# Four more half-size product groups, and a retention stage of four units per head, in a one-core decoder step

## The chip, the cores and the metric

The kernel runs on one core of a Trainium2 chip. The metric is the device time of one execution in microseconds (us), lower is better. In the names of the profile PE is the matrix engine (TensorE), PEld its weight loads, DVE the vector engine, ACT the scalar engine, POOL GpSimd and SP the engine whose queue issues most DMAs.

## What is computed

The reference is one inference step of a hybrid decoder layer for 1024 prompt tokens and 8 sample tokens (1032 token columns together), D_MODEL 1024. Cut to what matters here:

```python
hn   = rms_norm(x, norm_mix)
proj = hn @ w_in                                  # 7424 columns
rq, rk, rv, rg, aq, ak, av, gr, ga = split(proj)  # 512, 512, 1024, 1024, 3 x 768, 2 x 1024
# retention, 4 heads, keys of 128, values of 256, chunks of 128 tokens
for chunk: scores = (q @ k.T) * decay
           o  = scores @ v + (q @ state) * inner
           state = state * gamma**128 + (k * tail).T @ v
o = group_norm(o) * silu(rg)                      # per head, gates of 256 columns
r_branch = o @ w_ret_branch
# then dilated attention (3 groups), gated merge, output projection, SwiGLU FFN, final norm
```

The 8 samples do one retention step each, from a stored state of 128 x 256 per head, and that state is updated and written out.

## The kernel before

Activations lie transposed, features on the 128 partitions and 1032 tokens along the free axis. A product with a float32 weight is made of three fp32r products (high x high, high x low, low x high): POOL splits each weight into a high and a low part, ACT or DVE the activations.

Work on PE comes in two forms.

A **unit** (`unit`, L996) makes 128 output columns of a projection: 8 contraction steps k, each of 9 matmuls of 344 tokens, 72 matmuls. Two PSUM buffers `unit_ps` alternate, and so do two weight buffers. DVE takes a finished unit out of PSUM in `scaled` (times `rstd`), which frees the buffer (`unit_free`). POOL splits the weights of unit n (`split`, L864 and L867, 128x1024 each) when unit n-2 is done; SP loads them (`load`) when the split of unit n-2 is done.

A **half** (`in_half`, `product`, L1057) makes 256 output columns by seven products of half-size matrices instead of eight (Strassen-Winograd): 7 x 4 x 3 x 2 = 168 matmuls of 258 tokens. ACT snapshots and DVE combines the results into `temp` or `h_out`, DVE scales by `rstd`, SP stores 1032 KB to `att_spill`. IN_TURNS = 3 turns of two halves make the queries, keys and values of attention groups 0 and 1.

After the halves come the four units of U_HEAD0 (head 0: two of values, keys, queries), then four heads. Under head h six units run: values, keys and queries of head h+1 and the two units of head h's gates `rg`. Between their k steps PE does the **28 tasks** of head h's retention, placed by the table RET_AT: `(j, k): x` puts task x ahead of step k of unit j. Tasks by number: VT 0 to 3, VS 4 (values turned to token order), KT_ 5, 6, KS 7 (keys), SC 8, 9 (scores), UP 10 to 13 (state products), OUT_ 14 to 17 (outputs), OUTER 18 to 21 and OS 22 (samples), TURN 23 to 26 and TS 27 (outputs turned back). Tasks alternate between two PSUM banks: a task waits until the one two before it has been emptied (`task_free`), by ACT for VT, VS, KS, OUT_, OS, by DVE for the others. Instructions on an engine are executed in order, so a task that waits holds up the unit behind it.

DVE and ACT walk through `ret_slot(.., j)` for j = 0 to 5, each followed by taking unit j out. Of DVE's slots these matter:

- slot 1: scores, q times inner, then UP; slot 2 begins once `scaled` has taken unit 1, with UP+3 and then the **sample preparation**: casts s_khigh and s_vparts (L2217, L2219), s_klow, s_vparts (L2221, L2222), three s_kparts (L2225) and s_qmask (L2227), which signals `masked_ready`. PE's first OUTER task waits for it.
- slot 3: statistics and normalisation of the outputs (L2245 to L2260), which signals `normed` for TURN.
- slot 4: the turned outputs are copied into `wide`; in `gated` the two gate units are scaled into `stage`, put through Silu by ACT, and multiplied in (L2283).

ACT's slot 2 empties the four OUT_ tasks. The last head's tasks run in the six units of attention group 2 (U_GROUP2); there ACT does `spill(j)` after its slot j: it waits until DVE has taken unit j and issues a DMA.

The lines on which the order rests:

```python
RET_AT.update({(1, 0): 6, (1, 1): 7, (1, 2): 8, (1, 3): 9, (1, 5): 10, (1, 6): 11, (1, 7): 12, (2, 0): 13})
RET_AT.update({(2, 1 + j): 14 + j for j in range(7)})
RET_AT.update({(3, 0): 21, (3, 3): 22, (4, 4): 23, (4, 5): 24, (4, 6): 25, (4, 7): 26, (5, 1): 27})
```

Of the kernel before, what the change touches and what calls it, by code (L numbers as in the profile page):

```python
# [29 lines left out]
ALU = mybir.AluOpType  # L30
# [4 lines left out]
P = 128  # L35
# [30 lines left out]
U_HEADS = U_HEAD0 + 4  # L66
U_GROUP2 = U_HEADS + 6 * (HEADS - 1)
# [20 lines left out]
IN_TURNS = 3  # L88
# [45 lines left out]
RET_AT = {(0, 2 + j): j for j in range(6)}  # L134
RET_AT.update({(1, 0): 6, (1, 1): 7, (1, 2): 8, (1, 3): 9, (1, 5): 10, (1, 6): 11, (1, 7): 12, (2, 0): 13})
RET_AT.update({(2, 1 + j): 14 + j for j in range(7)})
RET_AT.update({(3, 0): 21, (3, 3): 22, (4, 4): 23, (4, 5): 24, (4, 6): 25, (4, 7): 26, (5, 1): 27})

STEPS_HEAD = 29
# [141 lines left out]
def build(nc, a, out):  # L281
    ctx = ExitStack()
    with ctx:
# [136 lines left out]
        att_spill = scratch("att_spill", [18, P, TOKENS])  # L420
# [49 lines left out]
        x_again = sem("x_again")  # L470
        window = sem("window")
# [86 lines left out]
        def in_columns(t, x):  # L558

            g, kind = divmod(2 * t + x, 3)  # L560
            return COL_ATT + KIND * kind + 2 * P * g, 6 * g + 2 * kind
# [28 lines left out]
        def _(sp):  # L590
# [43 lines left out]
            for t in range(IN_TURNS):  # L634
                if t == 1:
                    sp.dma_start(x_late[:], x_spill[0:KH, :, second].rearrange("k p t -> p k t")).then_inc(x_again, 16)
                for x in range(2):
                    half = 2 * t + x
                    sp.wait_ge(part_split, PRODUCTS * (half + 1))
                    if t + 1 < IN_TURNS:  # L640
                        in_load(x, (raw_a, raw_b)[x], t + 1)
                    elif x == 0:
                        for j, c in enumerate((COL_RV, COL_RV + P)):
                            load(Place(U_HEAD0), j, KT, w_in[:, :, c:c + P])
                    if half >= 1:
                        in_store(*IN_HALVES[half - 1])

            in_store(IN_TURNS - 1, 1)
            sp.wait_ge(product_done, LAST_IN + PRODUCTS)
            for j, c in enumerate((COL_RK, COL_RQ)):  # L650
                load(Place(U_HEAD0), 2 + j, KT, w_in[:, :, c:c + P])
# [3 lines left out]
            with sp.Fori(0, HEADS - 1) as h:  # L655
                for j, (c, by) in enumerate(((COL_RV + DV, DV), (COL_RV + DV + P, DV), (COL_RK + DK, DK),
                                             (COL_RQ + DK, DK), (COL_RG, DV), (COL_RG + P, DV))):
                    load(Place(U_HEADS, 6, h), j, KT, w_in[:, :, ds(h * by + c, P)])
            for j in range(6):
                c = COL_ATT + 2 * 256 + KIND * (j // 2) + P * (j % 2)  # L660
                load(Place(U_GROUP2), j, KT, w_in[:, :, c:c + P])
            for j in range(2):
                c = COL_RG + 3 * DV + P * j
                load(Place(U_GATE3), j, KT, w_in[:, :, c:c + P])
# [313 lines left out]
        def _(pe):  # L978
# [129 lines left out]
            for j in range(1, 4):  # L1108
                unit(Place(U_HEAD0), j, KT, a_hi, a_lo)


            def ret_task(pl, up, heads, j):


                ps = begin(pl, j)
                if j == 0:

                    pe.wait_ge(unit_free[0], up.half(0))
                    pe.wait_ge(unit_free[1], up.half(0))
# [44 lines left out]
                elif j == OS:  # L1164

                    taken(pl, OUTER + 3)
# [16 lines left out]
                end(mm, j)  # L1183

            def ret_stage(pl, up, heads):
                for j in range(6):
                    unit(up, j, KT, a_hi, a_lo,
                         between=lambda k: ret_task(pl, up, heads, RET_AT[j, k]) if (j, k) in RET_AT else None)

            with pe.Fori(0, HEADS - 1) as h:  # L1190
                ret_stage(Place(T_RET, RET_TASKS, h), Place(U_HEADS, 6, h), h)
            ret_stage(Place(T_RET + RET_TASKS * (HEADS - 1)), Place(U_GROUP2), HEADS - 1)

# [262 lines left out]
        def _(act):  # L1456
# [165 lines left out]
            def ret_slot(pl, h, j):  # L1622

                for x in {0: range(VT, KT_), 1: (KS,), 2: range(OUT_, OUTER), 3: (OS,)}.get(j, ()):
                    ps = full(pl, x)
# [11 lines left out]
                    empty(ins, x)  # L1637
                if j == 2:

                    act.wait_ge(task_free[1], pl.half(UP + 3) + 1)  # L1640
                    act.dma_start(out["p_ret"][0, 0][ds(h, 1)].rearrange("a d v -> d (a v)"), states[:, CHUNKS - 1, :])\
                       .then_inc(p_stored, 16)
                if j == 3:

                    act.wait_ge(task_free[0], pl.half(OUTER + 2) + 1)
                    act.wait_ge(task_free[1], pl.half(OUTER + 3) + 1)
# [7 lines left out]
            with act.Fori(0, HEADS - 1) as h:  # L1654
                pl = Place(T_RET, RET_TASKS, h)
                up = Place(U_HEADS, 6, h)
                for j in range(6):
                    ret_slot(pl, h, j)
                    if j >= 4:
                        in_place(up, j, ACT.Silu)  # L1660

                act.wait_ge(s_stored, h * 16 + 16)
                load_states(h + 1)
# [6 lines left out]
            for j in range(6):  # L1670
                ret_slot(Place(T_RET + RET_TASKS * (HEADS - 1)), HEADS - 1, j)
# [163 lines left out]
            act.dma_start(s_qkv_t[:], att_spill[:, :, SEQ:TOKENS].rearrange("a p t -> p a t")).then_inc(qkv_loaded, 16)  # L1835
# [198 lines left out]
        def _(dve):  # L2034
# [140 lines left out]
            scaled(Place(U_HEAD0), 0, v_t[:, 0, :])  # L2175
            scaled(Place(U_HEAD0), 1, v_t[:, 1, :])
            scaled(Place(U_HEAD0), 2, k_t[:])
            scaled(Place(U_HEAD0), 3, q_t[:], DK ** -0.5)
            dve.wait_ge(table_loaded, 16 * 2)

            def ret_slot(pl, h, j):

                if j < 2:

                    empty(dve.tensor_scalar(k_tok[:, 4 * j:4 * j + 4, :],
                                            full(pl, KT_ + j)[:].rearrange("p (q d) -> p q d", q=4),
                                            const("tail")[:, ds(h, 1)], None, ALU.mult), KT_ + j)
                if j == 1:
                    for x in range(2):
                        ps = full(pl, SC + x)[:].rearrange("p (q t) -> p q t", q=4)  # L2190
                        empty(dve.tensor_tensor(scores_t[:, 4 * x:4 * x + 4, :], ps,
                                                decay[:, ds(h, 1), :].to_broadcast([P, 4, P]), ALU.mult), SC + x)
# [3 lines left out]
                if j in (1, 2):  # L2196
                    for x in (range(UP, UP + 3) if j == 1 else (UP + 3,)):
                        ps = full(pl, x)
                        for q in range(2):
# [11 lines left out]
                            else:  # L2211
                                empty(ins, x)
                                dve.wait_ge(task_free[x % 2], pl.half(x) + 1)
                if j == 2:
                    dve.wait_ge(task_free[KS % 2], pl.half(KS) + 1)
# [14 lines left out]
                if j in (2, 3):  # L2230
                    for x in (range(OUTER, OUTER + 3) if j == 2 else (OUTER + 3,)):
                        if x == OUTER:
# [3 lines left out]
                        ps = full(pl, x)[:].rearrange("p (q d) -> p q d", q=2)  # L2236
                        empty(dve.scalar_tensor_tensor(out=s, in0=s, scalar=const("gamma")[:, ds(h, 1)], in1=ps,
                                                       op0=ALU.mult, op1=ALU.add), x)
                if j == 3:

                    for x in (OUT_ + 2, OUT_ + 3, OS):
                        dve.wait_ge(task_free[x % 2], pl.half(x) + 1)
# [19 lines left out]
                if j == 4:  # L2262

                    dve.wait_ge(p_stored, h * 16 + 16)

                    for x in range(4):
                        ps = full(pl, TURN + x)[:].rearrange("p (v t) -> p v t", v=2)
                        empty(dve.tensor_copy(wide[:, ds(h * 2, 2), 2 * P * x:2 * P * (x + 1)], ps), TURN + x)
                    ps = full(pl, TS)[:, 0:2 * SAMPLES].rearrange("p (v t) -> p v t", v=2)
                    empty(dve.tensor_copy(wide[:, ds(h * 2, 2), SEQ:TOKENS], ps), TS)  # L2270
# [4 lines left out]
            def gated(pl, j, h, v, done):  # L2275

                scaled(pl, j, stage[:, j % 2, :])
                dve.wait_ge(silu_done, done)

                for b in range(2):  # L2280
                    dve.wait_ge(task_free[b], h * (RET_TASKS // 2) + (T_RET + RET_TASKS) // 2)
                t = flat(wide[:, ds(h * 2 + v, 1), :])
                step(dve.tensor_tensor(t, t, stage[:, j % 2, :], ALU.mult))  # L2283

            with dve.Fori(0, HEADS - 1) as h:
                step.enter(h, STEPS_HEAD)
                up = Place(U_HEADS, 6, h)
                for j in range(6):
                    ret_slot(Place(T_RET, RET_TASKS, h), h, j)
# [4 lines left out]
                    elif j == 3:  # L2294
                        scaled(up, j, q_t[:], DK ** -0.5)
                    else:
                        gated(up, j, h, j - 4, h * 2 + (U_HEAD0 + j - 3))
                step.leave(HEADS - 1)

            for j in range(6):  # L2300
                ret_slot(Place(T_RET + RET_TASKS * (HEADS - 1)), HEADS - 1, j)
# [457 lines left out]
```

## Time and profile before

| what | value |
|---|---|
| time, median of 3 runs | 1776.24 us (1775.83 to 1776.53) |
| profiled execution, its own time | 1775.5 us |
| its span, first to last instruction | 1773.7 us |
| PE busy | 1749.7 us (99%) |
| DVE, ACT, POOL busy | 828.6, 496.8, 920.8 us |
| halves, 73 to 194.4 us | PE busy throughout |
| retention stage, 194.4 to about 600 us | PE busy throughout |

A start in a timeline is the first instruction's; matmuls overlap, so that a group's duration is longer than the distance to the next start. The distance between starts is what a step costs.

### The profile page before, as it was taken

Reading aid. Unit: us, or ns where it says so; the run is one execution under the profiler, and the core shown is the slowest. Engines: PE = TensorE matmul, PEld = TensorE weight load, DVE = VectorE, ACT = ScalarE, POOL = GpSimd, SP = SyncE. Lnnn points to the kernel's source line nnn. Section 1 sums busy time; section 2 is a strip of 40 time slices with the busy share of each in tenths; the row PEclk is TensorE's granted clock in tenths of the full one; section 3 lists DMA queues with packets and bytes.
Section 4 is the critical chain, followed back from the end, with each engine's and each line's share of the span. In section 5 each row is a group of like instructions: output and inputs, shape, how many; then the busy total and the mean of one; then the engine's idle time right before and its main releaser. Section 6 shows DMA issues by size and latency. Waiting matters only on the chain.

```text
span 1773.7 us, 29802 instructions
## 1 busy us (share of the span) xinstructions
PE 1749.7 (99%) x12362; PEld 1712.8 (97%) x12362; DVE 828.6 (47%) x909; ACT 496.8 (28%) x901; POOL 920.8 (52%) x492
## 2 busy tenths in 40 slices
PE   7999999999999999999999999999999999999998
PEld 6999999999999999999989999999999999999997
DVE  4633216353535254445837787444454444532213
ACT  6533101111111134656102235333333333201003
POOL 3697433333232332223437449988888886344550
PEclk9999999999999999999999999999999999999999
DMA  7332311212122414363733441222222222723112
GB/s 245 114 126 96 119 48 51 71 50 71 50 83 75 170 61 149 121 219 128 210 108 120 143 143 48 73 93 97 71 84 82 71 71 89 278 70 124 61 57 96
DMA packets 166947, 187.89 MB, mean 106 GB/s; under 512 B 7225, under 2 KB 143665, under 8 KB 166873
## 3 DMA queue, kind: packets, MB, share of 16 engines
q1 hardware_dynamic: 139008, 144.27, 25.3%
q10 hardware_dynamic: 27865, 42.56, 7.0%
q8 instruction: 55, 0.90, 0.2%
q14 instruction: 19, 0.16, 0.0%
HBM read 133.05 MB, written 53.76 MB: 105 GB/s over the span
## 4 chain that ended last, share of the span: by engine, by line
PE 49%; DVE 3%; DMA 1%; issue 0%; ACT 0%; DVEq 0%; SPq 0%
PE pair_ps L1057 25%; PE unit_ps L996 19%; PE unit_ps L1428 4%; DVE a_lo L2093 0%; DMA temp<-x_spill 0%; DVE temp L2563 0%; DVE s_lo L2093 0%; DVE wide L2597 0%; DMA x_spill<-temp 0%; DVE q_b L2387 0%; PE task_banks L1314 0%; DMA a_lo<-h_spill 0%; PE unit_ps L1437 0%; PE task_banks L1315 0%; DMA out_y_prompt<-y_row 0%
## 5 line engine op out<-in xcount | busy, mean ns | idle before, releaser
L996 PE MATMUL unit_ps<-a_hi,w_part 128*128 128x344 f32 x2976 | 600.7, 327 | 3.4 <-DVE a_lo L2079 3.0
L864 POOL TENSOR_TENSOR w_part<-w_raw,consts 128x1024 fp32r<-128x1024 f32 (+1 forms) x77 | 186.6, 2424 | 644.5 <-PE unit_ps L996 603.8
L996 PEld LDWEIGHTS unit_ps<-a_hi,w_part 128*128 128x128 f32 x2976 | 484.4, 189 | 12.6 <-issue 9.4
L996 PE MATMUL unit_ps<-a_lo,w_part 128*128 128x344 f32 x1488 | 315.5, 320 | 0.0
L996 PEld LDWEIGHTS unit_ps<-a_lo,w_part 128*128 128x128 f32 x1488 | 251.1, 189 | 0.0
L1057 PE MATMUL pair_ps<-a_hi,slots_a 128*128 128x258 f32 x1344 | 225.8, 283 | 1.1 <-DVE a_lo L2093 1.1
L867 POOL TENSOR_TENSOR w_part<-w_raw,w_part 128x1024 fp32r<-128x1024 f32 (+1 forms) x79 | 208.8, 2643 | 15.7 <-DVE a_lo L2079 9.7
L1057 PEld LDWEIGHTS pair_ps<-a_hi,slots_a 128*128 128x128 f32 x1344 | 189.2, 190 | 1.3 <-DVE a_lo L2093 1.3
L996 PE MATMUL unit_ps<-b_hi,w_part 128*128 128x344 f32 x720 | 133.4, 320 | 0.0
L1057 PE MATMUL pair_ps<-a_lo,slots_b 128*128 128x258 f32 x672 | 122.2, 284 | 0.0
L1529 ACT ACTIVATE snap<-pair_ps 128x516 f32<-128x516 f32 x112 | 67.4, 602 | 185.2 <-PE pair_ps L1057 185.2
L2102 DVE TENSOR_TENSOR h_out<-pair_ps,snap 128x516 f32<-128x516 f32 x56 | 38.8, 694 | 170.8 <-ACT snap L1529 111.2
L996 PEld LDWEIGHTS unit_ps<-b_hi,w_part 128*128 128x128 f32 x720 | 117.0, 188 | 0.3 <-DVE gate_a L2515 0.3
L2102 DVE TENSOR_TENSOR temp<-pair_ps,snap 128x516 f32<-128x516 f32 x56 | 38.8, 695 | 130.0 <-ACT snap L1529 76.0
L1057 PEld LDWEIGHTS pair_ps<-a_lo,slots_b 128*128 128x128 f32 x672 | 98.7, 190 | 0.0
L880 POOL TENSOR_TENSOR slots_b<-mixed,slots_b 128x512 fp32r<-128x512 f32 x56 | 77.9, 1395 | 27.3 <-ACT slots_b L1520 27.2
L1057 PE MATMUL pair_ps<-a_lo,slots_a 128*128 128x258 f32 x448 | 90.5, 284 | 0.0
L1057 PE MATMUL pair_ps<-s_lo,slots_b 128*128 128x258 f32 x448 | 90.5, 283 | 0.0
L1057 PE MATMUL pair_ps<-s_lo,slots_a 128*128 128x258 f32 x448 | 90.4, 283 | 0.0
L880 POOL TENSOR_TENSOR slots_a<-mixed,slots_a 128x512 fp32r<-128x512 f32 x56 | 74.1, 1323 | 18.6 <-ACT slots_a L1520 18.5
L1057 PE MATMUL pair_ps<-s_hi,slots_a 128*128 128x258 f32 x448 | 78.3, 287 | 0.8 <-issue 0.8
L1057 PE MATMUL pair_ps<-s_hi,slots_b 128*128 128x258 f32 x448 | 77.0, 283 | 0.0
(283 smaller groups left out, 2890.8 us busy)
## 6 DMA issues: line engine op xcount, KB each, us to landing
w_raw<-in_w_in SPq DMA_DIRECT2D x46, 512.0 KB, 3.7
h_spill<-h_out SPq DMA_DIRECT2D x11, 1032.0 KB, 4.9
raw_a<-in_w_gate_up SPq DMA_DIRECT2D x11, 1024.0 KB, 6.9
raw_b<-in_w_gate_up SPq DMA_DIRECT2D x11, 1024.0 KB, 5.1
gate_spill<-stage ACTq DMA_DIRECT2D x16, 516.0 KB, 2.9
a_lo<-h_spill SPq DMA_DIRECT2D x15, 516.0 KB, 5.3
w_raw<-in_w_down SPq DMA_DIRECT2D x16, 448.0 KB, 3.5
att_in<-att_spill ACTq DMA_DIRECT2D x3, 2048.0 KB, 9.3
```

The costliest lines, as they stand in the source:

```text
L864: pool.tensor_tensor(part[:, 0], raw, one, ALU.mult).then_inc(w_high, 1)
L867: pool.tensor_tensor(part[:, 1], raw, part[:, 0].bitcast(F32), ALU.subtract).then_inc(w_split, 1)
L880: pool.tensor_tensor(part_slot(s)[:, 1], source(s, raw), part_slot(s)[:, 0].bitcast(F32), ALU.subtract).then_inc(part_split, 1)
L996: mm = pe.matmul(unit_ps[s][:, n, 0:PIECE], w_part[:, slot, w, k0 + by * k, :], x[:, k, n * PIECE:(n + 1) * PIECE], start=(k == 0 and part ...
L1057: mm = pe.matmul(ps[:, n, 0:QUAD], part_slot(s)[:, w, k, :], a[:, n * QUAD:(n + 1) * QUAD], start=(k == 0 and part == 0 and not more), sto ...
L1428: mm = pe.matmul(unit_ps[s][:, n, 0:c.stop - c.start], weights[:, w, k, :], x[:, k, c], start=(k == 0 and part == 0), stop=(k == nf - 1 an ...
L1529: act.activation(halves(snap[:, i, :]), ps[:, :, 0:QUAD], ACT.Copy).then_inc(snap_done, 1)
L2102: dve.tensor_tensor(halves(out[:, b, h]), ps[:, :, 0:QUAD], halves(snap[:, i, :]), ALU.add).then_inc(combined, 1)
```

## The change

IN_TURNS becomes 5, so that four more halves run: head 0's values and the gates `rg` of heads 0, 1 and 2, all stored to `att_spill`. U_HEAD0 keeps two units (keys, queries). SP loads the values back into `v_t` when the products are done, and each head's gates into the last two rows of `wide` (`rg_load`). Heads 0 to 2 have four units each; RET_AT is more closely packed, and the outputs of head h are turned in unit 0 of head h+1 (TURN_AT). Gates get their Silu in ACT's slot 0 and are multiplied in by DVE in slot 2 of the next head, between the sample preparation and the OUTER updates. The loops over heads are written out, and numbers of tasks come from a table, RET_NUMBER. The last head keeps its six units, with the new RET_AT.

```diff
-U_HEADS = U_HEAD0 + 4
-U_GROUP2 = U_HEADS + 6 * (HEADS - 1)
+U_HEADS = U_HEAD0 + 2
+U_GROUP2 = U_HEADS + 4 * (HEADS - 1)
-IN_TURNS = 3
+IN_TURNS = 5
...
+RET_AT = {(0, 1): (0, 1), (0, 2): (2, 3), (0, 3): (4, 5), (0, 4): (6, 7), (0, 7): (8,), (1, 0): (9,)}
+RET_AT.update({(1, 2 + j): (UP + j,) for j in range(4)})
+RET_AT.update({(1, 6): (OUT_,), (1, 7): (OUT_ + 1,), (2, 0): (OUT_ + 2,), (2, 1): (OUT_ + 3,)})
+RET_AT.update({(2, 3 + j): (OUTER + j,) for j in range(4)})
+RET_AT[3, 1] = (OS,)
+
+TURN_AT = {(0, 5): (TURN, TURN + 1), (0, 6): (TURN + 2, TURN + 3), (0, 7): (TS,)}
+TURN_LAST = {(4, 4): (TURN,), (4, 5): (TURN + 1,), (4, 6): (TURN + 2,), (4, 7): (TURN + 3,), (5, 1): (TS,)}
...
 # SP
+            def rg_load(h):
+
+                stored_by(ATT_HALVES + 1 + h)
+                wait(sp, gated_rows, 2 * h)
+                at = SPILL_RG + 2 * h
+                sp.dma_start(wide[:, KT - 2:KT, :], att_spill[at:at + 2].rearrange("f p t -> p f t")).then_inc(rg_loaded, 16)
+
+            sp.wait_ge(product_done, LAST_IN + PRODUCTS)
+            stored_by(ATT_HALVES)
+            sp.dma_start(v_t[:], att_spill[SPILL_RV:SPILL_RV + 2].rearrange("f p t -> p f t")).then_inc(v_loaded, 16)
             in_store(IN_TURNS - 1, 1)
...
+            for h in range(HEADS - 1):
+                n = h + 1
+                for j, c in enumerate((COL_RV + DV * n, COL_RV + DV * n + P, COL_RK + DK * n, COL_RQ + DK * n)):
+                    load(Place(U_HEADS + 4 * h), j, KT, w_in[:, :, c:c + P])
+                    if j == 1 and h != 1:
+                        rg_load(h // 2)
...
 # ACT
-                for x in {0: range(VT, KT_), 1: (KS,), 2: range(OUT_, OUTER), 3: (OS,)}.get(j, ()):
+                for x in {0: (*range(VT, KT_), KS), 2: range(OUT_, OUTER), 3: (OS,)}.get(j, ()):
...
+                if j == 0 and h:
+
+                    act.wait_ge(rg_loaded, 16 * h)
+                    for v in range(2):
+                        row = wide[:, KT - 2 + v, :]
+                        act.activation(row, row, ACT.Silu).then_inc(silu_done, 1)
...
             for j in range(6):
-                ret_slot(Place(T_RET + RET_TASKS * (HEADS - 1)), HEADS - 1, j)
+                ret_slot(HEADS - 1, j)
                 spill(Place(U_GROUP2), j, att_spill[12 + j])
...
 # DVE
+                if j == 0:
+
+                    for x in range(2):
+                        empty(dve.tensor_scalar(k_tok[:, 4 * x:4 * x + 4, :], ...
+                    if h:
+                        ret_turned(h - 1)
                 if j < 2:
+                    ps = own(SC + j)[:].rearrange("p (q t) -> p q t", q=4)
...
                 if j == 1:
...
-                if j in (1, 2):
-                    for x in (range(UP, UP + 3) if j == 1 else (UP + 3,)):
+                    for x in range(UP, UP + 4):
...
                 if j == 2:
...
-                if j in (2, 3):
-                    for x in (range(OUTER, OUTER + 3) if j == 2 else (OUTER + 3,)):
+                if j == 2:
+                    if h:
+                        gated(h - 1)
+                    for x in range(OUTER, OUTER + 4):
...
+            def gated(h):
+
+                dve.wait_ge(silu_done, U_HEAD0 + 2 * (h + 1))
+                for x in range(TURN, TS + 1):
+                    at = RET_NUMBER[h, x]
+                    dve.wait_ge(task_free[at % 2], Place(T_RET).half(at) + 1)
+                for v in range(2):
+                    t = wide[:, 2 * h + v, :]
+                    dve.tensor_tensor(t, t, wide[:, KT - 2 + v, :], ALU.mult).then_inc(gated_rows, 1)
```

## Rows read from the trace of the kernel before

**Rows 1.** The page, part 1: busy us (share of the span) xinstructions.

```profile
PE 1749.7 (99%) x12362; PEld 1712.8 (97%) x12362; DVE 828.6 (47%) x909; ACT 496.8 (28%) x901; POOL 920.8 (52%) x492
```

**Rows 2.** Windows: the halves, and head 0; us, each engine's busy us, PEclk, DMA.

```profile
73.00:195.00 122.00, 122.00 (x1013) 122.00 (x1013) 41.81 (x40) 40.60 (x70) 99.30 (x66) 1.00 0.30 101
240.80:330.50 89.70, 89.70 (x566) 85.52 (x565) 40.55 (x69) 9.92 (x16) 28.49 (x13) 1.00 0.16 49
```

**Rows 3.** Timeline of PE: first half, first unit of U_HEAD0.

```profile
72.99 0.40 PE L1057 MATMUL pair_ps<-a_hi,slots_a 128*128 128x258 f32 x2
...
194.43 0.63 PE L996 MATMUL unit_ps<-a_hi,w_part 128*128 128x344 f32 x3
```

**Rows 4.** The chain that ended last: FFN halves, and a wake of PE.

```profile
896.80 0.14 issue
...
1087.97 413.48 PE pair_ps L1057 x3432
```

**Rows 5.** Timeline of DVE: units 0 and 3 of U_HEAD0 taken out.

```profile
206.06 1.23 DVE L2054 TENSOR_TENSOR v_t<-unit_ps,rstd 128x1032 f32<-128x1032 f32 x1 [1.07 <-PE unit_ps L996]
...
240.09 1.23 DVE L2056 SCALAR_TENSOR_TENSOR q_t<-unit_ps,rstd 128x1032 f32<-128x1032 f32 x1 [10.13 <-PE unit_ps L996]
```

**Rows 6.** Timeline of PE, head 1: UP+3, OUT_+1, OUT_+2, OUTER.

```profile
359.84 1.03 PE L1145 MATMUL task_banks<-v_tok,k_tok 128*128 128x256 f32 x4
...
364.82 0.59 PE L1152 MATMUL task_banks<-v_tok,scores_t 128*128 128x256 f32 x2
...
367.95 0.59 PE L1152 MATMUL task_banks<-v_tok,scores_t 128*128 128x256 f32 x2
...
374.23 0.40 PE L1162 MATMUL task_banks<-s_vparts,s_kparts 72*128 72x256 f32 x2
```

**Rows 7.** Timeline of DVE, head 1: unit 1 taken out, slots 2 and 3.

```profile
360.04 1.23 DVE L2054 TENSOR_TENSOR v_t<-unit_ps,rstd 128x1032 f32<-128x1032 f32 x1 [0.42 <-PE unit_ps L996]
361.19 0.99 DVE L2205 SCALAR_TENSOR_TENSOR states<-states,consts,task_banks 128x256 f32<-128x256 f32 x2
362.21 0.34 DVE L2217 CAST s_khigh<-s_ktok 8x128 fp32r<-8x128 f32 x1
362.48 2.67 DVE L2219 CAST s_vparts<-s_vtok 8x256 fp32r<-8x256 f32 x2
...
369.61 0.23 DVE L2227 TENSOR_TENSOR s_qmask<-q_t,consts 128x64 f32<-128x64 f32 x1
374.78 0.75 DVE L2237 SCALAR_TENSOR_TENSOR s_state<-s_state,consts,task_banks 128x512 f32<-128x512 f32 x1 [4.95 <-PE task_banks L1162]
...
387.85 2.71 DVE L2245 BATCH_NORM_STATS2 stats<-o_tok 128x6 f32<-128x256 f32 x8 [6.57 <-ACT s_otok L1636]
...
399.70 1.21 DVE L2056 SCALAR_TENSOR_TENSOR q_t<-unit_ps,rstd 128x1032 f32<-128x1032 f32 x1
```

**Rows 8.** Timeline of POOL, head 1: the split after unit 1.

```profile
360.09 2.39 POOL L864 TENSOR_TENSOR w_part<-w_raw,consts 128x1024 fp32r<-128x1024 f32 x1 [11.41 <-PE unit_ps L996]
362.56 2.45 POOL L867 TENSOR_TENSOR w_part<-w_raw,w_part 128x1024 fp32r<-128x1024 f32 x1
```

**Rows 9.** Source line of the two s_vparts casts: duration ns min/median/max, all heads.

```profile
L2219 DVE CAST s_vparts<-s_vtok x8: 273/1318/2365, 272.6 to 542.6; 8x256 fp32r<-8x256 f32 x8
```

**Rows 10.** Timelines of PE, DVE, ACT, last head, end of unit 1.

```profile
539.65 1.03 PE L1145 MATMUL task_banks<-v_tok,k_tok 128*128 128x256 f32 x4
...
539.95 1.23 DVE L2054 TENSOR_TENSOR stage<-unit_ps,rstd 128x1032 f32<-128x1032 f32 x1 [0.45 <-PE unit_ps L996]
...
541.22 0.34 ACTq L1668 DMA_DIRECT2D att_spill<-stage  x1
543.42 0.60 ACT L1634 ACTIVATE o_tok<-task_banks 128x512 f32<-128x512 f32 x1 [17.60 <-PE task_banks L1154]
```

**Rows 11.** Source line of the gate product: duration ns min/median/max.

```profile
L2283 DVE TENSOR_TENSOR wide<-wide,stage x6: 1232/1342/1451, 322.5 to 512.3; 128x1032 f32 x6
```

**Rows 12.** DMA issues, 190 to 215 us: count, KB each, median us to landing.

```profile
w_raw<-in_w_in SPq DMA_DIRECT2D x3, 512.0 KB, 6.7
```

More of the change, by code:

```diff
@@ L470, in build @@
         x_again = sem("x_again")
+        v_loaded = sem("v_loaded")
+        rg_loaded = sem("rg_loaded")
+        gated_rows = sem("gated_rows")
         window = sem("window")
@@ L1107, in _, with ret_task @@
             pe.wait_ge(combined, COMBOS * 2 * IN_TURNS)
[L1108 to L1115, printed above, removed]
+            unit(Place(U_HEAD0), 1, KT, a_hi, a_lo)
+            def ret_task(up, heads, j):
+                pl, at = Place(T_RET), RET_NUMBER[heads, j]
+                ps = begin(pl, at)
                 if j == 0:
+                    if heads:
+                        pe.wait_ge(unit_free[0], up.half(0) - 1)
+                        pe.wait_ge(unit_free[1], up.half(0) - 1)
+                    else:
+                        pe.wait_ge(v_loaded, 16)
+                if j == KT_:
                     pe.wait_ge(unit_free[0], up.half(0))
+                if j == SC:
                     pe.wait_ge(unit_free[1], up.half(0))
@@ L1164, in ret_task @@
                 elif j == OS:
-                    taken(pl, OUTER + 3)
+                    taken(pl, RET_NUMBER[heads, OUTER + 3])
                     for n in range(SAMPLES):
@@ L1182, in ret_task, with ret_tasks, between @@
                                        ident[0:SAMPLES, 0:SAMPLES], start=True, stop=True)
[L1183 to L1192, printed above, removed]
+                end(mm, at)
+            def ret_tasks(up, h, j):
+                def between(k):
+                    if h and (j, k) in TURN_AT:
+                        for x in TURN_AT[j, k]:
+                            ret_task(up, h - 1, x)
+                    for x in RET_AT.get((j, k), ()):
+                        ret_task(up, h, x)
+                    if h == HEADS - 1:
+                        for x in TURN_LAST.get((j, k), ()):
+                            ret_task(up, h, x)
+                return between
+            for h in range(HEADS):
+                up = Place(U_HEADS + 4 * h)
+                for j in range(4 if h < HEADS - 1 else 6):
+                    unit(up, j, KT, a_hi, a_lo, between=ret_tasks(up, h, j))
             def turn_keys(g, i):
@@ L1652, in ret_slot @@
                                    bias=const("eps", SAMPLES)[:, 1:2]).then_inc(root, 1)
[L1654 to L1660, printed above, removed]
+            for h in range(HEADS - 1):
+                for j in range(4):
+                    ret_slot(h, j)
                 act.wait_ge(s_stored, h * 16 + 16)
@@ L2174, in _, with ret_slot, own, emptied @@
             step.settle()
[L2175 to L2178, printed above, removed]
+            scaled(Place(U_HEAD0), 0, k_t[:])
+            scaled(Place(U_HEAD0), 1, q_t[:], DK ** -0.5)
             dve.wait_ge(table_loaded, 16 * 2)
-            def ret_slot(pl, h, j):
+            def ret_slot(h, j):
+                pl = Place(T_RET)
+                def own(x):
+                    return full(pl, RET_NUMBER[h, x])
+                def emptied(x):
+                    at = RET_NUMBER[h, x]
+                    dve.wait_ge(task_free[at % 2], pl.half(at) + 1)
+                if j == 0:
+                    for x in range(2):
+                        empty(dve.tensor_scalar(k_tok[:, 4 * x:4 * x + 4, :],
+                                                own(KT_ + x)[:].rearrange("p (q d) -> p q d", q=4),
+                                                const("tail")[:, ds(h, 1)], None, ALU.mult), RET_NUMBER[h, KT_ + x])
+                    if h:
+                        ret_turned(h - 1)
@@ L2188, in ret_slot @@
                 if j == 1:
[L2189 to L2192, printed above, removed]
                     q = q_t[:, 0:SEQ].rearrange("p (n t) -> p n t", t=P)
                     dve.tensor_tensor(q, q, inner[:, ds(h, 1), :].to_broadcast([P, CHUNKS, P]), ALU.mult).then_inc(q_ready, 1)
-                if j in (1, 2):
-                    for x in (range(UP, UP + 3) if j == 1 else (UP + 3,)):
-                        ps = full(pl, x)
+                    wait(dve, p_stored, h * 16)
@@ L2261, in ret_slot, with ret_turned @@
                     ins.then_inc(normed, 1)
[L2262 to L2270, printed above, removed]
+            def ret_turned(h):
+                pl = Place(T_RET)
+                rows = wide[:, 2 * h:2 * h + 2, :]
+                for x in range(4):
+                    at = RET_NUMBER[h, TURN + x]
+                    ps = full(pl, at)[:].rearrange("p (v t) -> p v t", v=2)
+                    empty(dve.tensor_copy(rows[:, :, 2 * P * x:2 * P * (x + 1)], ps), at)
+                at = RET_NUMBER[h, TS]
+                ps = full(pl, at)[:, 0:2 * SAMPLES].rearrange("p (v t) -> p v t", v=2)
+                empty(dve.tensor_copy(rows[:, :, SEQ:TOKENS], ps), at)
@@ L2272, in masks8 @@
             def masks8():
                 return const("ident", SAMPLES)[:, 0:SAMPLES].unsqueeze(2)
[L2275 to L2289, printed above, removed]
+            def gated(h):
+                dve.wait_ge(silu_done, U_HEAD0 + 2 * (h + 1))
+                for x in range(TURN, TS + 1):
+                    at = RET_NUMBER[h, x]
+                    dve.wait_ge(task_free[at % 2], Place(T_RET).half(at) + 1)
+                for v in range(2):
+                    t = wide[:, 2 * h + v, :]
+                    dve.tensor_tensor(t, t, wide[:, KT - 2 + v, :], ALU.mult).then_inc(gated_rows, 1)
@@ L2290, in _ @@
+            for h in range(HEADS - 1):
+                up = Place(U_HEADS + 4 * h)
+                for j in range(4):
+                    ret_slot(h, j)
                     if j < 2:
```

85 lines of the change are left out of this document (49 added, 36 removed).

## The prediction, made before the result was known

> **What bounds the kernel now.** I read the page's busy times first: PE is busy 99% of the span, no other engine over 52% [rows 1]. Then the windows: in the halves (73 to 195 us) and in each head PE is busy for the whole stretch, at full clock, with DVE at less than half of a head and POOL at a third [rows 2]. So in the stages that change PE alone sets the time. Each microsecond of matmuls taken away is won, each microsecond for which the in-order PE waits is lost at once, and the others matter only where PE waits for them. Then the timelines, for the price of a unit and of a half, and for where DVE, ACT and POOL stand when PE will ask.
>
> **What it removes and adds on PE.** Two values units and six gate units go. Between the starts of `scaled` for units 0 and 3 of U_HEAD0 lie 34.03 us, 11.34 us a unit [rows 5]; a k step of nine matmuls is 1.42 us, and eight of them 11.36, which I take. Eight units: 90.9 us. Four halves come. The six of before begin at 72.99 and end at 194.43: 20.24 us each [rows 3]. That this holds over more turns is shown by the FFN's halves, 3432 matmuls in 413.48 us, 0.1205 us each, 168 of them 20.24 us [rows 4]. Four: 81.0 us. The 112 tasks stay, in number and kind. **Gain on PE: 9.9 us**, if PE never waits.
>
> **The first wait: the sample preparation.** Call the end of a head's unit 1 zero; in head 1 of before it is 359.84, where the UP+3 that stands ahead of unit 2 starts [rows 6]. Before, PE does one UP, four OUT_ and five k steps until its first OUTER at 374.23, 14.39 later. DVE is ready at 369.61 + 0.23 = 369.84, that is 10.0 [rows 7]: 4.4 us of slack. In the new table only OUT_+2, OUT_+3 and three k steps lie between. An OUT_ with its k step takes 367.95 - 364.82 = 3.13 [rows 6], so OUTER is reached at 2 x 3.13 + 1.42 = 7.7.
>
> When is the preparation done then? It still begins only when unit 1 has been taken out. It loses the pair of UP updates ahead of it (361.19 to 362.2, 1.0 us), so with equal durations it ends at 9.0. But look at its casts. The two s_vparts casts have one shape and take 0.27 and 2.37 us [rows 9]; the long one ends at 362.48 + 2.67 = 365.15, just behind the end of POOL's second split instruction, 362.56 + 2.45 = 365.01 [rows 7, 8]. Those two POOL instructions are let go by the same end of unit 1, and they run from 0.25 to 5.2 whatever the head. If DVE's casts wait for them, starting 1.0 us earlier buys nothing: s_khigh, now at 1.4, lies inside the first POOL instruction (to 2.64), and the rest is again held until 5.2. Then the end stays at 10.0, or goes to 10.3, if POOL's second instruction also gets ahead of the first cast.
>
> The Trainium skill, page "SBUF — State Buffer", section "SBUF: two separate sides", says that vector and GpSimd instructions with such operands take one shared port pair as an exclusive lock, whichever starts first, for the whole instruction. The 2.37 us of the cast agrees. By the rule the wait below is 2.45 us a head, without it 1.45.
>
> I take 10.0. PE starts a matmul some 0.15 us after a late release (issue 0.14 in the chain) [rows 4]. **Stall: 10.0 + 0.15 - 7.7 = 2.45 us**, bounds 1.45 (end at 9.0) and 2.8 (end at 10.3). Three heads (0, 1, 2): 7.4 us.
>
> **The second wait, in the last head.** There ACT's `spill(1)` stands between slot 0 and slot 2, and slot 2 empties the OUT_ tasks. Before, the first OUT_ is done about two k steps after unit 1, and the spill, issued at 541.22, is out of the way; the first copy is at 543.42 [rows 10]. Now OUT_ and OUT_+1 are done inside unit 1, and OUT_+2 at zero needs the bank of OUT_. ACT is then waiting for DVE's take of unit 1 (539.95 + 1.23 = 541.18), issues the DMA (0.34 from 541.22), then copies for 0.60: 542.2, and PE starts at 542.35, against 539.65 wanted: **2.7 us** [rows 10]. Bounds 2.5 and 3.0. OUTER would then be reached at 2.7 + 7.7 = 10.4, behind the preparation's 10.15: the first wait is hidden by the second in this head. In heads 0 to 2 nothing stands between ACT's slots, and it costs nothing.
>
> **What I cost at nothing.**
> - `gated` now stands between the preparation and the updates of s_state. Two products of 1.23 to 1.45 us [rows 11], overlapped a little, and an update of 0.75 [rows 7] end 3.2 to 3.6 after `masked_ready`. PE, woken 0.15 after it, needs that bank for OUTER+2 two OUTER steps (1.66 each, 0.24 over a k step) later, at 3.5. Between nothing and 0.15 a head; I take nothing.
> - OS moves from (3, 3) to (3, 1). Slot 3 of DVE takes 399.70 - 387.85 = 11.85 us [rows 7] and starts two k steps earlier, while TURN, moved to step 5 of the next head, comes about 24 us after unit 3 began: `normed` is up some 6 us before. The q product and the packed VT, KT_ and TURN pairs have their bank emptied in 0.6 to 0.75 us, against a k step of 1.42.
> - Removing the loops: PE shows no gap in a head [rows 2], so nothing is won.
> - SP: the v_t load (1 MB) is now ahead of the last store, and two tables are ahead of the weights of the first values unit. Split by POOL in 4.9 us, these are wanted by PE 22.7 us after the products end: they may land up to 17.8 us after it. Weight loads of this stretch land 6.7 us after their issue [rows 12]; issued some 5 to 9 us after the products' end, the new ones are there by about 16, an estimate. The `rg_load` that waits for `gated_rows` holds SP until about 12.7 of a unit-1 end; behind it is the weight load of unit 2 of the next head, wanted more than 40 us later. Hidden by two units in flight; without that cover each microsecond late costs one, once.
> - The extra ACT, DVE and POOL work of four halves is that of the six before, in which PE never waits.
>
> **The sum.** -9.9 + 3 x 2.45 + 2.7 = +0.2 us; with a little for the bounds, of which the upper is nearer, +0.3. The profiled execution took 1775.5 us (span 1773.7, 1.8 around it), the median of the runs is 0.7 above it. So 1775.8 in its own time, and 1776.5 against the median. By the bounds: -9.9 + 3 x 1.45 + 2.5 = -3.1, and -9.9 + 3 x (2.8 + 0.15) + 3.0 = +1.9. Own range of this case: 1773.1 to 1778.2.
>
> **Rivals.** A measurement of this kernel can tell about 0.2%, 3.5 us.
> - *POOL does not hold the casts*, DVE goes first each time: the second cast costs 0.27 instead of 2.37 and the preparation ends near 6.9, before PE asks. The last head's wait alone is left: -9.9 + 2.7 = -7.2, 1769.0. For it: once POOL's instruction is the longer one. Against: all four heads have one long cast [rows 9]. Chance 0.12.
> - *DVE gets its 1.0 us*, end at 9.0: -9.9 + 3 x 1.45 + 2.7 = -2.8, 1773.4. Chance 0.08, within 0.2%.
> - *No wait binds*, the full 9.9 us: 1766.3. It needs `masked_ready` 2.3 us sooner and ACT's copies ahead of the spill; no row offers that. Chance 0.04.
> - *Slower: `gated` holds the state updates.* If Silu or the loaded gates come late in slot 2, DVE waits ahead of the OUTER updates, and PE at OUTER+2, in heads 1, 2 and 3. 1.2 us late each: +0.3 + 3.6, 1780.1. It decides from 1.1 us on. For it: the chain SP, DMA, ACT, DVE is new. Against: the gates are asked for a whole head ahead. Chance 0.08.
> - A slack that I have misjudged anywhere in the packed table repeats in three or four heads; 1.2 us each give 1781. Chance 0.10.
>
> **Chances and range.** My case 0.58. Within 0.2%: 0.58 + 0.08 = 0.66; faster 0.12 + 0.04 = 0.16; slower 0.18. The range of 8 in 10 leaves out the two fast cases (0.16) and the far end of the last: 1772.5 to 1781.0.
>
> **What would show it.** Four more halves at 20.24 us, the first unit of U_HEAD0 at about 275.4, heads 0 to 2 about 69.4 us apart (45.4 of units, 21.5 of tasks, which is the 89.7 of a head before [rows 2] less six units, and 2.45 of wait). Idle PE ahead of the first OUTER (L1162), released by DVE s_qmask, about 2.4 us in heads 0 to 2 and none in the last; there idle PE ahead of OUT_+2 (L1152), released by ACT's o_tok copy, 2.7. A long cast again, ending with POOL's second instruction. The prediction is wrong if the preparation ends before 9 after unit 1, if ACT's copy in the last head is not behind the spill, or if PE idles elsewhere in the stage.

## The result

The changed kernel takes 1778.82 us (median of 20 runs, 1776.76 to 1782.64), the kernel before 1776.10 beside it (20 runs). The ratio is 1.0017, with an interval of 1.0010 to 1.0024: 2.7 us slower, inside the 0.2% that the prediction calls the same, and inside its range. Forecast were 1776.5 us. One execution, of the run e5_fill further down, took 6841 us at a mean granted clock of 0.24; every median leaves it out.

The page of the changed kernel, part 1, against [rows 1]: PE is busy for 4.6 us less and the span is 3.6 us longer, so PE stands idle for 8.2 us more. Line numbers are those of the changed kernel: L1207 is the line that was L1162 before, L1197 was L1152.

```profile
PE 1745.1 (98%) x12458; PEld 1706.3 (96%) x12458; DVE 836.1 (47%) x925; ACT 517.8 (29%) x942; POOL 946.2 (53%) x520
```

Who made PE wait between 60 and 600 us, where before it never did: engine, line, what was waited for, us in total, times, longest.

```profile
PE task_banks L1207 <- DVE s_qmask L2301: 6.7, 3, 2.2
PE task_banks L1197 <- ACT o_tok L1690: 2.5, 1, 2.5
```

These are the two waits of the prediction, and there is no other of any size. L1207 is the first OUTER task of heads 0 to 2, L1197 is OUT_+2 of the last head.

**The first wait**, in head 1. Timeline of PE: OUT_+2 at the end of unit 1, then OUTER behind its wait (in brackets: idle time and releaser).

```profile
402.21 0.59 PE L1197 MATMUL task_banks<-v_tok,scores_t 128*128 128x256 f32 x2
...
412.32 0.47 PE L1207 MATMUL task_banks<-s_vparts,s_kparts 72*128 72x256 f32 x2 [2.24 <-DVE s_qmask L2301]
```

Timeline of DVE over the same stretch, to be held against [rows 7]:

```profile
402.48 1.23 DVE L2117 TENSOR_TENSOR v_t<-unit_ps,rstd 128x1032 f32<-128x1032 f32 x1 [6.27 <-PE unit_ps L1035]
403.63 1.28 DVE L2291 CAST s_khigh<-s_ktok 8x128 fp32r<-8x128 f32 x1
404.84 2.64 DVE L2293 CAST s_vparts<-s_vtok 8x256 fp32r<-8x256 f32 x2
...
411.94 0.23 DVE L2301 TENSOR_TENSOR s_qmask<-q_t,consts 128x64 f32<-128x64 f32 x1
412.08 1.23 DVE L2361 TENSOR_TENSOR wide<-wide 128x1032 f32<-128x1032 f32 x1
```

And POOL's split, let go by the same end of unit 1, as in [rows 8]:

```profile
402.46 2.38 POOL L903 TENSOR_TENSOR w_part<-w_raw,consts 128x1024 fp32r<-128x1024 f32 x1 [13.01 <-PE unit_ps L1035]
404.92 2.42 POOL L906 TENSOR_TENSOR w_part<-w_raw,w_part 128x1024 fp32r<-128x1024 f32 x1
```

With 402.21 as zero the preparation ends at 412.17 - 402.21 = 9.96, as it did before at 10.0, although it begins 1.0 us earlier. The cast s_khigh, 0.34 us before, now takes 1.28: it is issued at 403.63, inside POOL's first instruction, and ends with it at 404.84 to 404.91. The casts behind it again take 2.64 together and end at 407.48, just behind POOL's second (407.34). PE starts 0.15 us after s_qmask.

**The second wait**, in the last head. Timeline of PE, then of ACT:

```profile
545.94 0.67 PE L1197 MATMUL task_banks<-v_tok,scores_t 128*128 128x256 f32 x2 [2.53 <-ACT o_tok L1690]
```

```profile
544.81 0.34 ACTq L1731 DMA_DIRECT2D att_spill<-stage  x1
545.20 1.09 ACT L1690 ACTIVATE o_tok<-task_banks 128x512 f32<-128x512 f32 x2 [25.93 <-DVE stage L2117]
```

The copies of two OUT_ tasks stand behind the spill, which waited for DVE's take of unit 1. ACT stands idle for 25.93 us ahead of its copies, the last part of it with both outputs ready in PSUM.

**What no step of the prediction had.** Windows of the changed kernel: busy us of each engine, then the granted clock of TensorE (PEclk), DMA share, GB/s.

```profile
410.00:412.30 2.30, 0.08 (x1) 0.01 (x1) 2.27 (x4) 0.00 (x0) 0.00 (x0) 1.00 0.26 78
413.50:417.50 4.00, 4.00 (x19) 4.00 (x18) 2.27 (x3) 0.00 (x0) 0.00 (x0) 0.57 0.49 124
414.00:416.00 2.00, 2.00 (x9) 2.00 (x8) 1.77 (x3) 0.00 (x0) 0.00 (x0) 0.50 0.41 33
...
543.00:546.00 3.00, 0.47 (x4) 0.21 (x2) 2.45 (x3) 0.80 (x2) 2.43 (x2) 1.00 0.13 52
546.00:550.50 4.50, 4.50 (x16) 4.04 (x17) 4.38 (x6) 0.88 (x2) 2.33 (x1) 0.62 0.35 124
548.00:550.00 2.00, 2.00 (x8) 1.86 (x7) 1.92 (x4) 0.60 (x1) 0.33 (x1) 0.50 0.09 25
```

Some 1 to 2 us after PE has gone on from its idle 2.2 and 2.5 us the granted clock falls from 1.00 to 0.50 of full speed, that is from 2.4 to 1.2 GHz, for some 3 to 4 us, and comes back. It shows in the distance of PE's starts: three matmuls of 344 tokens take 0.87 us instead of 0.47.

```profile
414.62 1.06 PE L1035 MATMUL unit_ps<-a_hi,w_part 128*128 128x344 f32 x3
415.49 1.06 PE L1035 MATMUL unit_ps<-a_lo,w_part 128*128 128x344 f32 x3
...
417.48 0.64 PE L1035 MATMUL unit_ps<-a_hi,w_part 128*128 128x344 f32 x3
417.95 0.63 PE L1035 MATMUL unit_ps<-a_lo,w_part 128*128 128x344 f32 x3
```

Its price can be read from DVE's takes of unit 1, one in each head (they are L2117's, at 332.75, 402.48, 473.77 and 543.55): the heads are 69.73, 71.29 and 69.78 us apart, so the slow stretch of head 1 costs 1.5 us. In the last head the first OUTER starts at 555.31, 9.37 us after OUT_+2. In the run e5_fill, whose last head has the same wait and no fall behind it, this takes 550.95 - 543.18 = 7.77: the fall costs 1.6 us.

### The profile page after: what moved, and what is told of

Read it like the earlier page. It is cut to its first block, busy times and chain, and to the rows that moved or that the text cites. A ratio compares the mean times of both kernels' runs of the same rounds, so it can differ in the third digit from the quotient of the medians.

```text
span 1777.3 us, 29822 instructions
## 1 busy us (share of the span) xinstructions
PE 1745.1 (98%) x12458; PEld 1706.3 (96%) x12458; DVE 836.1 (47%) x925; ACT 517.8 (29%) x942; POOL 946.2 (53%) x520
## 4 chain that ended last, share of the span: by engine, by line
PE 90%; DVE 5%; DMA 2%; ACT 1%; issue 1%; POOL 1%; DVEq 0%; ACTq 0%; SPq 0%
PE unit_ps L1035 41%; PE pair_ps L1096 35%; PE unit_ps L1482 4%; PE task_banks L1316 2%; PE task_banks L1289 1%; PE task_banks L1302 1%; PE task_banks L1213 1%; PE task_banks L1190 1%; DVE s_kparts L2299 1%; DMA temp<-x_spill 1%; DVE s_lo L2156 1%; PE task_banks L1197 1%; DVE temp L2640 0%; DVE a_lo L2156 0%; PE task_banks L1185 0%
## 5 line engine op out<-in xcount | busy, mean ns | idle before, releaser
L1035 PE MATMUL unit_ps<-a_hi,w_part 128*128 128x344 f32 x2592 | 526.3, 328 | 3.9 <-DVE a_lo L2142 3.5
L903 POOL TENSOR_TENSOR w_part<-w_raw,consts 128x1024 fp32r<-128x1024 f32 (+1 forms) x69 | 166.3, 2410 | 607.3 <-PE unit_ps L1035 551.0
L1035 PEld LDWEIGHTS unit_ps<-a_hi,w_part 128*128 128x128 f32 x2592 | 424.4, 189 | 12.9 <-issue 9.9
L1035 PE MATMUL unit_ps<-a_lo,w_part 128*128 128x344 f32 x1296 | 276.2, 322 | 0.0
L1096 PE MATMUL pair_ps<-a_hi,slots_a 128*128 128x258 f32 x1536 | 258.1, 283 | 1.6 <-DVE a_lo L2156 1.3
L1035 PEld LDWEIGHTS unit_ps<-a_lo,w_part 128*128 128x128 f32 x1296 | 219.8, 190 | 0.0
L1096 PEld LDWEIGHTS pair_ps<-a_hi,slots_a 128*128 128x128 f32 x1536 | 216.1, 190 | 2.0 <-DVE a_lo L2156 1.5
L906 POOL TENSOR_TENSOR w_part<-w_raw,w_part 128x1024 fp32r<-128x1024 f32 (+1 forms) x71 | 189.7, 2672 | 15.0 <-DVE a_lo L2142 9.7
L1096 PE MATMUL pair_ps<-a_lo,slots_b 128*128 128x258 f32 x768 | 139.8, 284 | 0.5 <-issue 0.3
L1096 PEld LDWEIGHTS pair_ps<-a_lo,slots_b 128*128 128x128 f32 x768 | 112.8, 190 | 0.8 <-issue 0.5
```

Of the source, the lines that this page charges most:

```text
L903: pool.tensor_tensor(part[:, 0], raw, one, ALU.mult).then_inc(w_high, 1)
L906: pool.tensor_tensor(part[:, 1], raw, part[:, 0].bitcast(F32), ALU.subtract).then_inc(w_split, 1)
L1035: mm = pe.matmul(unit_ps[s][:, n, 0:PIECE], w_part[:, slot, w, k0 + by * k, :], x[:, k, n * PIECE:(n + 1) * PIECE], start=(k == 0 and part ...
L1096: mm = pe.matmul(ps[:, n, 0:QUAD], part_slot(s)[:, w, k, :], a[:, n * QUAD:(n + 1) * QUAD], start=(k == 0 and part == 0 and not more), sto ...
```

## The experiments

Each edit is to the changed kernel. The runs were made on three chips, each with the kernel before beside them on the same chip (1776.2 to 1776.4 us, against 1776.1 in the result above). The change itself did not run again beside them, so a distance to its 1778.8 us is good to some tenths only. There are 5 executions each of e1, e3, e3_again and e7, and 11 each of the others.

| run | median us | ratio to before (interval) | PE waits over 0.5 us in the stage | at half clock in the profile |
|---|---|---|---|---|
| the change | 1778.82 | 1.0017 (1.0010 to 1.0024) | 3 x 2.2, 2.5 | heads 1 and 3 |
| e1_outer_later | 1767.66 | 0.9956 (0.9942 to 0.9969) | 2.5 | none |
| e2_copies_first | 1778.75 | 1.0018 (1.0009 to 1.0027) | 4 x 2.2 | heads 1 and 2 |
| e3_both | 1765.59 | 0.9945 (0.9931 to 0.9958) | none | none |
| e4_split_after | 1772.23 | 0.9976 (0.9967 to 0.9985) | 2.5, 2 x 0.9 | head 3 |
| e5_fill | 1776.52 | 1.0003 (0.9994 to 1.0011) | 2.5 | none |
| e6_one_step | 1772.64 | 0.9977 (0.9968 to 0.9986) | 2.5, 3 x 0.8 | head 3 |
| e7_split_after_gates | 1765.48 | 0.9938 (0.9924 to 0.9951) | none | none |
| e3_again | 1765.33 | 0.9941 (0.9928 to 0.9955) | none | none |

### OUTER two steps later

```diff
-RET_AT.update({(2, 3 + j): (OUTER + j,) for j in range(4)})
-RET_AT[3, 1] = (OS,)
+RET_AT.update({(2, 5): (OUTER,), (2, 6): (OUTER + 1,), (2, 7): (OUTER + 2,), (3, 0): (OUTER + 3,)})
+RET_AT[3, 2] = (OS,)
```

> The four OUTER tasks two k steps later (from step 5 of unit 2), OS one later. If the wait for the sample preparation is a matter of the table alone, PE reaches OUTER at 10.5 us after unit 1 instead of 7.7, behind the preparation's 10.15: the idle time of PE ahead of L1207 goes from 6.7 us to under 0.5, the time falls by 7.2 us and by the slow-clock stretch that followed the wait in head 1 (1.5 us) : 1778.8 to about 1770.5. The last head keeps its 2.7 us and its slow clock. Rival, the preparation is itself paced by something that PE's later tasks free (it moves with them): PE still waits about 2 us a head and the time stays at 1778.

Measured 1767.66 us, 11.2 less than the change, against 8.3 expected. The waits for s_qmask are gone, so the table alone made them. The last head kept its wait, and in this profile no slow stretch followed it:

```profile
PE task_banks L1197 <- ACT o_tok L1690: 2.5, 1, 2.5
```

I had taken the slow clock of one profile for a constant. With three fewer waits there are fewer occasions for it, which is where part of the 2.9 us more than expected most likely is; that isn't shown. For the profiled executions there is a second part: here the halves begin at 71.59, in the change at 73.02, ahead of all that the edit touches. Over the ten profiles this start lies between 71.6 and 73.2.

### The copies ahead of the spill

```diff
+                early = 2 if h == HEADS - 1 else 0
-                for x in {0: (*range(VT, KT_), KS), 2: range(OUT_, OUTER), 3: (OS,)}.get(j, ()):
+                for x in {0: (*range(VT, KT_), KS), 1: range(OUT_, OUT_ + early), 2: range(OUT_ + early, OUTER), 3: (OS,)}.get(j, ()):
```

> In the last head ACT empties OUT_ and OUT_+1 ahead of its spill of unit 1. If the spill order is what PE waits for, the 2.5 us of idle ahead of OUT_+2 vanish, and the preparation's wait, hidden in this head until now, comes up in their place with 2.4 us: the time moves by 0.3 us, or by up to 2 where the slow clock does not follow the new wait. Rival, the two waits add and are not nested: 2.7 us and the slow clock's 1.7 are won, 1774.5.

Measured 1778.75, no change. The waits of this kernel:

```profile
PE task_banks L1207 <- DVE s_qmask L2302: 9.0, 4, 2.2
```

One wait has taken the place of the other: four times s_qmask instead of three, and none for o_tok. The nested pair of the prediction is shown. Taking one away is worth nothing as long as the other stands.

### Both edits

> Both edits. If the four waits and the slow clock behind them are all that stands between the change and its gain on PE, the whole 9.9 us appear: 1776.1 - 9.9 = 1766.2 us, up to 0.6 more for the small hitch in the halves, and PE idle in the retention stage under 0.5 us. Rival, the halves or the written-out loops cost something too, which the waits hid: 1768 to 1770.

Measured 1765.59, and 1765.33 when it ran again: 10.6 and 11.1 us below the kernel before. No wait is left in the stage, and the heads stand 67.3 us apart (takes of unit 1 by DVE):

```profile
331.40 1.23 DVE L2118 TENSOR_TENSOR v_t<-unit_ps,rstd 128x1032 f32<-128x1032 f32 x1 [6.27 <-PE unit_ps L1035]
...
398.70 1.23 DVE L2118 TENSOR_TENSOR v_t<-unit_ps,rstd 128x1032 f32<-128x1032 f32 x1 [6.27 <-PE unit_ps L1035]
```

67.3 against 69.73 prices one wait at 2.43 us, where 2.45 were forecast. The first FFN stretch of the chain, which stood at 1087.97 [rows 4], stands here at

```profile
1077.44 413.48 PE pair_ps L1096 x3432
```

10.5 us earlier. But 1.2 of them were there before the halves began, ahead of all that was changed. The first half, before and in this run:

```profile
72.99 0.40 PE L1057 MATMUL pair_ps<-a_hi,slots_a 128*128 128x258 f32 x2
```

```profile
71.75 0.40 PE L1096 MATMUL pair_ps<-a_hi,slots_a 128*128 128x258 f32 x2
```

From there to the FFN stretch the gain is 9.3 us, not 9.9; it is 9.1 in e3_again and 9.4 in e7, which begins its halves at 72.96. Of what is missing, 0.3 us is in the halves: they take 202.73 us here, and exactly the forecast 202.40 in the profiles of e1 and e6. So the halves and the written-out loops cost little: 0.8 us at most.

> The kernel with both edits once more, on the same chip as the one beside it: 1765.6 us, so that the two repairs can be compared; without a wait in the stage there should be no stretch at the lower clock in heads.

### POOL's split behind the preparation

```diff
+            for n in range(U_HEAD0 + 2, U_GROUP2 + 4, 2):
+                for j in range(2):
+                    if (n + j - U_HEADS) % 4 == 3:
+                        pool.wait_ge(masked_ready, (n + j - U_HEADS) // 4 + 1)
+                    split(Place(n), j, KT)
...
```

> The task table as in the change, but POOL's split that the end of unit 1 lets go waits for masked_ready as well. If POOL's two instructions hold the casts, the preparation runs through without a 2.4 us cast, is ready 6.9 to 7.1 us after unit 1 instead of 10.0, and PE finds it ready at 7.7: three waits gone, about 1778.8 - 7.2 - 1.5 = 1770, the last head's wait for the copies stays. Rival, the long cast is DVE's own (its partitions, its write): its 2.35 us stay, the preparation ends at 10 and the time stays at 1778 or above.

Measured 1772.23. The casts with POOL out of the way, duration in ns min/median/max over all heads, against [rows 9]:

```profile
L2298 DVE CAST s_vparts<-s_vtok x8: 274/278/285, 334.1 to 538.5; 8x256 fp32r<-8x256 f32 x8
```

No long cast is left, and PE no longer waits for s_qmask. In head 1 the preparation ends 6.6 us after DVE's take of unit 1 begins (406.62 - 400.06), in the change 9.7 (412.17 - 402.48). The preparation's stretch at 10.0 was POOL's doing. But the split now begins when the gate products do, and these suffer. Timelines of DVE and of POOL in head 1:

```profile
406.39 0.23 DVE L2306 TENSOR_TENSOR s_qmask<-q_t,consts 128x64 f32<-128x64 f32 x1
406.54 4.57 DVE L2366 TENSOR_TENSOR wide<-wide 128x1032 f32<-128x1032 f32 x2
```

```profile
406.70 3.32 POOL L903 TENSOR_TENSOR w_part<-w_raw,consts 128x1024 fp32r<-128x1024 f32 x1 [19.62 <-DVE s_qmask L2306]
410.09 3.25 POOL L906 TENSOR_TENSOR w_part<-w_raw,w_part 128x1024 fp32r<-128x1024 f32 x1
```

The two products take 4.57 us together instead of 2.37, POOL's instructions 3.3 each instead of 2.4. The times fit one order, worked out and not seen: product, POOL, product, POOL, each waiting for the one ahead. The state updates behind the products come late, and PE waits for them, which is the place of the slower rival, with another cause. So the median stays 2.2 us above the expected 1770. The waits for the updates:

```profile
PE task_banks L1212 <- DVE s_state L2318: 1.7, 2, 0.9
```

### The same, behind the gate products too, with the copies first

The edit of e4 with one more line, and the edit of e2. The added line:

```diff
                         pool.wait_ge(masked_ready, (n + j - U_HEADS) // 4 + 1)
+                        wait(pool, gated_rows, 2 * ((n + j - U_HEADS) // 4))
```

> The task table of the change, with POOL's split after unit 1 made to wait for the preparation and for the gate products of DVE's slot 2 too, and with the copies ahead of the spill in the last head. In the run in which the split waited for the preparation alone, the gate products then took 4.57 us beside POOL instead of 2.37, and PE waited 0.9 us for a state update in two heads. If POOL and DVE standing in each other's way, and the spill, are all there is, no wait is left in the stage: the split ends about 14.5 us after unit 1, ahead of its use, and the time is that of the run with both edits, 1765.6, within 1 us. Rival, the packed table has a further wait that the first ones hid (or the late split is now itself waited for): 1768 or more.

Measured 1765.48, beside 1765.33 of the other repair on the same chip. No wait is left in the stage, so the densely packed table of the change hid no further one. Both repairs have the copies first; for the other wait one changes PE's table and one POOL's order, and they end at the same time.

### OUTER one step later

```diff
-RET_AT.update({(2, 3 + j): (OUTER + j,) for j in range(4)})
+RET_AT.update({(2, 4 + j): (OUTER + j,) for j in range(4)})
```

> OUTER one k step later only (from step 4 of unit 2). PE reaches it at 9.1 us after unit 1, the preparation's end stays at 10.0: the wait shrinks from 2.4 to about 1.0 us in heads 0 to 2. If the wait costs its length alone, 4.3 us are won, 1774.5; if a short wait spares the slow clock too, 1.5 more, 1773. The last head keeps its wait.

Measured 1772.64, below both figures by little. The waits shrink by 1.4 us each, one k step:

```profile
PE task_banks L1207 <- DVE s_qmask L2301: 2.5, 3, 0.8
```

None of these short waits is followed by a slow stretch; the last head's 2.5 us is, in the profile. Over the eleven executions time goes with the mean granted clock: it is 0.997 or 0.998 in the four of 1770.3 to 1771.0 us and 0.995 or 0.996 in the seven of 1772.6 to 1774.2. That the fall behind the last head's wait divides them is likely and not shown.

### PE kept busy while it waits

```diff
                     if j == OUTER:
+                        for _ in range(5 if heads < HEADS - 1 else 0):
+                            pe.matmul(ps[:, 0:DV], k_tok[:, 0, :], v_tok[:, 0, :], start=True, stop=True)
                         pe.wait_ge(masked_ready, heads + 1)
```

> The table as in the change, but in heads 0 to 2 PE does five float32 matmuls of 256 columns (2.15 us, thrown away by the start of the real product) in the bank of the first OUTER task before it waits for the preparation. The output is the same. If an idle PE is what makes the granted clock fall behind the wait, the time of these heads is about 69.8 us each and none has a stretch at a lower clock: 1.5 us less than the change where it fell in one head, 1777.3. If the clock falls for another reason (a rhythm in time, the heat of the stage), head 1 or another shows its slow stretch all the same, and the time stays at 1778.8.

Measured 1776.52, ratio 1.0003 against the change's 1.0017. PE in head 0, where five useless products fill the wait and OUTER starts as late as ever:

```profile
339.12 2.32 PE L1206 MATMUL task_banks<-v_tok,k_tok 128*128 128x256 f32 x10
341.43 0.51 PE L1209 MATMUL task_banks<-s_vparts,s_kparts 72*128 72x256 f32 x2
```

No head has a stretch at the lower clock in this profile, and the median is 2.3 us lower though OUTER starts no earlier in any head. The heads are 69.7 us apart, all three. That is the share of the clock, within what medians of separate sessions can tell. The executions agree: the granted clock is 0.9963 in the mean of these eleven, 0.9944 in the mean of the change's twenty and 0.9965 over the 53 of the kernel before that ran beside the experiments. The fill is in heads 0 to 2, so the last head's fall can still come.

## Why the prediction was right, and where it was not

- **The gain on PE**, 9.9 us from eight units out and four halves in: right in the main. With every wait away the medians are 10.6 to 11.1 us below the kernel before; in the profiles 9.1 to 9.4 us are gained between the first half and the FFN, and the rest of the distance lies ahead of the halves or in the spread.
- **The sample preparation as first wait**, 2.45 us in heads 0 to 2: right in place and size (2.43, from the heads' distances), and so is its reason. e4 shows that the late end is POOL's hold on the casts. The lock that the Trainium skill states in "SBUF — State Buffer", section "SBUF: two separate sides", gave 2.45 us, and the traces agree: cast and POOL instruction end together, at 404.91 and 404.84. The forecast distance of heads, 69.4 us, was a little short by a misread row: the 89.7 us taken for a head of before is the length of the window asked for, and DVE's takes of unit 1, at 360.04 and 449.95, are 89.9 apart. With that it is 69.6, and 69.7 were measured.
- **The copies behind the spill**, 2.7 us in the last head, hiding the first wait there: right. OUT_+2 starts at 545.94, 2.7 us late, and e2 shows the nesting.
- **Costed at nothing:** no other wait came in the stage. The weights behind the longer burst were there at 288.3, 12.3 us after the products' end at 276.0, against 17.8 allowed. `normed`, the TURN pairs and `rg_load` never held PE.
- **Where it failed: the sum.** It priced a wait at its length. Waits of 2.2 to 2.7 us also cost the clock that comes after, 1.5 and 1.6 us in the profiled execution and about 2.3 us on the median (e5). No term of the sum stood for it. For the profiled executions: -9.9 + 7.3 of waits for the preparation + 2.7 + 3.1 of clock = +3.2, and the spans differ by 3.6. On the median +0.3 was forecast and +2.7 measured; the clock is nearly all of the difference. The bounds of the likeliest case reached 1778.2 and did not hold 1778.8. The wide range did, but for other reasons than this one: it was widened for a misjudged slack in the packed table, which never came. That it held for a cost that it had no term for is luck.

The rival that POOL does not hold the casts, and the one that DVE gets its 1.0 us, are ruled out by the 1.28 us of s_khigh and by the preparation's end at 9.96. The slower rival, DVE's updates behind `gated`, did not come in the change; e4 shows what it takes.

## What to carry to other kernels

When work is taken from the engine that sets the time, redo the slack of everything that the shorter stage now asks for: here 9.9 us of products were gained and about 10 lost to two waits. The ends of the chains behind them had not moved, only their due times had. Put an instruction that waits for late work (a spill) behind those that other engines need, and look for instructions that two engines start on the same event before moving either. Where the matrix engine sets the time, price an idle gap above its length. When two waits are nested, repair both before judging either.

## What the runs showed of the hardware

**The clock behind a short wait.** Counting the profiles of the change, e1, e2, e4, e5 and e6, PE stood idle in the retention stage for 2.2 to 2.5 us twelve times. Six of them were followed by a fall of the granted clock to half, none of the five gaps of 0.8 to 0.9 us was, and no fall came in the stage without a gap ahead of it (the kernel before, e3 in two profiles, e7). Whether a gap of 2.2 us is followed by a fall differs between the same heads of kernels that do the same up to there (the change fell in head 1 only, e2 in heads 1 and 2); what decides it stays open.

Outside the stage even shorter gaps have a fall behind them. Where the FFN's halves begin, every one of the ten profiles has PE idle for 1.1 to 1.7 us and, 1.8 us later, for 0.8. In the kernel before:

```profile
1062.45 0.51 PE L1057 MATMUL pair_ps<-a_hi,slots_a 128*128 128x258 f32 x2 [1.07 <-DVE a_lo L2093]
1064.24 0.48 PE L1057 MATMUL pair_ps<-s_hi,slots_a 128*128 128x258 f32 x2 [0.81 <-issue]
```

```profile
1064.00:1068.00 4.00, 3.75 (x20) 3.79 (x21) 4.00 (x3) 2.97 (x4) 4.00 (x4) 0.62 0.02 6
```

Six of the ten fell behind this pair (before, e1, e2, e5, e6, e7), the change, both e3 and e4 did not. There a fall costs less than in the heads. From the 1064.24 of the second row to PE's first product with slots_b, at 1071.62, pass 7.38 us; in e3, without a fall, 6.85, and in that stretch PE waits 0.5 us for others. Further on even that is gone: from a unit's take by DVE ahead of it (988.16 before) to one behind the FFN's halves (1541.93) pass 553.8 to 554.7 us with the fall and 553.9 to 554.4 without. DVE and POOL are busy throughout the 4 us of the window shown, so most likely PE does not set the time there as it does in the heads. The Trainium skill, "TensorE: Matmul & The Clock Gate", section "What's actually happening", says that idleness of the array closes its clock gate to 1.2 GHz and activity opens it to 2.4. The two levels and the order, idle first and the fall behind it, agree with these rows.

**DVE and POOL taking turns.** Where both have such instructions queued, neither goes through first with all of its own: in e4 two DVE products and two POOL instructions, which take 2.37 us (the change) and 4.8 us (e7) with the other engine out of the way, took 4.57 and 6.6 beside each other. A small cast pays what is left of POOL's instruction: 2.37 us instead of 0.27 for one that is issued just behind the start of POOL's, 1.28 instead of 0.20 (e4) for one issued in its middle.
